# A third bank for the transposes' ring while the samples attend

## The chip, the cores and the metric

The kernel runs on one core of a Trainium2 chip. The metric is the device time of one execution in microseconds (us). Before the change three runs took 1328.84 to 1329.03 us, median 1329.01.

## The reference

One decoder layer for a prompt of 512 tokens and for 8 samples of 8 new tokens each, with shared weights and float32 throughout. What the change touches is the samples' attention over their caches: three groups of 8 heads with 64 columns, whose keys lie 1, 4 and 16 positions apart (`DILS`), so that every query sees at most 129 keys of its group.

```python
def dilated_attn_sample(q, k_new, v_new, k_buf, v_buf, dil, slopes):
    kc = jnp.concatenate([k_buf, k_new], axis=1)
    vc = jnp.concatenate([v_buf, v_new], axis=1)
    idx = buf + jnp.arange(t)[:, None] - dil * j[None, :]
    kg, vg = kc[:, idx], vc[:, idx]
    scores = jnp.einsum('bthd,btjhd->bhtj', q, kg) * (dh ** -0.5)
    scores = scores - slopes * (dil * j)
    m = jnp.max(scores, axis=-1)
    p = jnp.exp(scores - m)
    o = jnp.einsum('bhtj,btjhd->bthd', p, vg) / den
    ...
# layer:  h = adaLN-RMSNorm(x; c);  [q,k,v | u,v | gA,gB] = h @ w_in
#         A = attention of the three groups, combined by their softmax denominators
#         x = x + gate1(c) * ((sig(gA) * A @ w_pa + sig(gB) * B @ w_pb) @ w_o)
#         x = x + gate2(c) * HierMoE(adaLN-RMSNorm(x; c));  y = adaLN-RMSNorm(x; c_final)
```

## The kernel before, in words

The order of every engine's work is written out by hand, engine by engine, and semaphores tie the engines together. The stages are: adaLN and the first norm; the projections v, u, gb and pb; for each of the three head groups q, k and values of the prompt with the prompt's attention; the attention of the eight samples; the gates ga0 and ga1; pa and wo; routing; the experts; the final norm. Between the prompt's groups TensorE also computes rows of the modulation (`ada_step`, line 997) into a PSUM bank of their own, bank 5 (`ada_bank`). Their last rows (G = 3) are read by VectorE (`ada_rows`, line 2039 on) in the third group of the prompt's attention. After that bank 5 isn't used until `routed(0)` puts the first tile's routing logits there, after the samples' attention, the gates, pa and wo; later it serves `keep_warm` and the experts.

The other PSUM banks belong to two rings (`Ring`, line 176): `mm`, banks 0 to 4, for products, and `tp`, banks 6 and 7, for transposes. A ring's uses are listed ahead of the program (`stage`), each with the engine that empties it; use m has bank m modulo the number of banks. TensorE waits with `wait_empty` until the use that had the bank before, two uses back in `tp`, is emptied.

**The loads.** SyncE issues a stream of loads into four slots of 2 MB each (`SLOTS`), one load after the other in the stream's order, each when what last read its slot is done (`wait_slot_read`). For the samples the stream goes: keys of sample b in two slots (the first with 5 tiles of 128 keys in two DMAs, 256 KB and 1 MB; the second with 8 tiles in one DMA of 2 MB), then values of sample b - 1 in the same manner. The first key slot is free when key tile 4 is transposed, the second when key tile 12 is, both value slots when the previous sample's values product is done.

**The loop of the samples' attention** (line 1303 on) has ten rounds; round b takes the scores of sample b and the values of sample b - 1. `scores(b)` turns 13 key tiles (`turn_keys`, four 128x128 transposes each, recorded under line 970) and interleaves them with four score products (`quad_scores`, line 1253): key tiles 0 to 2, product 0 (key 0), tiles 3 to 6, product 1 (keys 1 to 4), tiles 7 to 10, product 2 (keys 5 to 8), the transposes of the previous sample's exponentials (lines 1235 and 1237), tiles 11 and 12, the heads of sample b - 2 (`gather_heads`, line 1299), product 3 (keys 9 to 12). `attend(b - 1)` follows (lines 1284, 1286 and 1291). In rounds 1 to 4 a tile of the prompt's output is transposed at the round's end (line 970, copied out by ScalarE at line 1546); a wait for VectorE's `combine` stands before it.

```python
            def scores(b):
                lead = (3, 7, 11, 13)
                x = 0
                for quad in range(4):
                    while x < lead[quad]:
                        if b and x == PT_AT:
                            turn_exponentials(b - 1)
                        turn_keys(b, x)
                        x += 1
                    if quad == 3 and b >= 2:
                        gather_heads(b - 2)
                    quad_scores(b, quad)
```

ScalarE copies the even key tiles out of their bank (line 169, with a small copy of the new keys ahead, line 163), VectorE the odd ones (lines 171 and 165). VectorE also places the exponentials (lines 2127 to 2130), adds the bias and takes the maxima (line 2156 on), and in rounds 1 to 4 has one step of the prompt's combination (lines 2098 to 2102) behind each of its first five key tiles. In round 0 it combines the prompt's denominators (line 2080 on), for which it waits for partial results that GpSimd loads back from DRAM (line 853). The copied key tiles stand in a ring of ten in SBUF (`KT_SLOTS`).

Of the kernel before, what the change touches and what calls it, by code (L numbers as in the profile page):

```python
# [175 lines left out]
class Ring:  # L176
# [3 lines left out]
    def __init__(self, banks, filled, emptied_act, emptied_dve):  # L180
        self.banks, self.filled = banks, filled
        self.emptied = {"act": emptied_act, "dve": emptied_dve}
        self.users, self.first = [], {}

    def stage(self, name, uses, user):
        self.first[name] = len(self.users)
        self.users += [user] * uses

    def bank(self, m):
        return self.banks[m % len(self.banks)]  # L190

    def wait_empty(self, pe, m):

        if m >= len(self.banks):
            self.wait_emptied(pe, m - len(self.banks))

    def wait_emptied(self, eng, m):

# [12 lines left out]
def build(nc, t, out):  # L211

    ctx = ExitStack()
    with ctx:
        def sem(name):
            return ctx.enter_context(nc.semaphore(name))
# [15 lines left out]
        psum = ctx.enter_context(nc.psum_tensor("psum", [P, 8, CH], F32))  # L232
# [120 lines left out]
        def rt(start, *shape):  # L353
            return at(RT0 + start, *shape)
# [8 lines left out]
        earlier, nth = rt(780, TILES + 1, 16), rt(880, TILES, 16)  # L363
# [35 lines left out]
        tp_filled, tp_act, tp_dve = sem("tp_filled"), sem("tp_act"), sem("tp_dve")  # L399
# [5 lines left out]
        ada_read, ada_out = sem("ada_read"), sem("ada_out")  # L405
# [46 lines left out]

        mm = Ring([psum[:, b, :] for b in range(5)], mm_filled, mm_act, mm_dve)
        ada_bank = psum[:, 5, :]
        tp = Ring([psum[:, b, :] for b in (6, 7)], tp_filled, tp_act, tp_dve)
        tp.stage("c", 2, "dve")
        tp.stage("h", 2 * TILES, "act")
        tp.stage("mod", 1, "dve")
# [24 lines left out]
                    mm.stage(f"o{g}{i - 2}", 1, "dve")  # L483
        PT_AT = 11
        KT_USER = ["act", "dve"] * 6 + ["act"]
        for b in range(NB + 2):
            if b < NB:
                for x in range(XT):
                    if b and x == PT_AT:
                        tp.stage(f"pt{b - 1}", 1, "dve")  # L490
                    tp.stage(f"kt{b}x{x}", 1, KT_USER[x])
                mm.stage(f"ss{b}", 1, "dve")
            if b >= 2:
                tp.stage(f"ot{b - 2}", 1, "act")
            if b == NB:
                mm.stage("ga0", TILES, "act")
                tp.stage(f"pt{b - 1}", 1, "dve")
            if 1 <= b <= NB:
                mm.stage(f"so{b - 1}", 1, "dve")
            if 1 <= b <= 4:  # L500
                tp.stage(f"o{b - 1}", 1, "act")
        mm.stage("ga1", TILES, "act")
        mm.stage("pa", 2 * TILES, "dve")
        tp.stage("shift", 3, "dve")
        tp.stage("mix", 2 * TILES, "dve")
        mm.stage("wo", 2 * TILES, "dve")
# [452 lines left out]
        def _(pe):  # L959
            used = [0]  # L960
# [53 lines left out]
            def samples_product(name, j, lhs, half):  # L1014

                n = S0[name][2 * j + half]
                slot_wait(n)
                raw, _, _ = half_slot(n)
                m = bank_of(name, j, 4)
                if half == 0:  # L1020
                    mm.wait_empty(pe, m)
                for k in range(4):
                    for out_, cols in quarters(m):
                        ins = nc.tensor.matmul(out_, lhs[:, 4 * half + k, :], raw[:, k, cols],  # L1024
                                               start=(half == 0 and k == 0), stop=(half == 1 and k == 3))
                ins.then_inc(samples_read if half == 0 else mm_filled, 1)
# [46 lines left out]
            for k in range(KD):  # L1073
                ada_step(0, k)
                if k >= KD - TILES:
                    i = k - (KD - TILES)
# [35 lines left out]
            m = tp.first["rep"]  # L1112
# [7 lines left out]
            for i in range(TILES):  # L1120
                pe.wait_ge(vn_done, i + 1)
                for half in range(2):
                    m = mm.first["sgu"] + 2 * i + half
# [134 lines left out]
# [12 lines that stand above are left out]
# [24 lines left out]
            def gather_heads(b):  # L1294
                u = tp.first[f"ot{b}"]
                mm.wait_emptied(pe, mm.first[f"so{b}"])
                tp.wait_empty(pe, u)
                for j in range(4):
                    ins = nc.tensor.matmul(tp.bank(u)[:, j * NT:(j + 1) * NT], om[:, j * P:(j + 1) * P],
                                           c_("seltok"), start=True, stop=True)  # L1300
                ins.then_inc(tp_filled, 1)

            for b in range(NB + 2):
                if b < NB:
                    scores(b)
                if b == NB:
                    samples_product("ga0", 0, h4_raw, 0)
                if b >= NB:
                    gather_heads(b - 2)
                if b == NB:  # L1310
                    samples_product("ga0", 0, h4_raw, 1)
                    project("ga0", H_PARTS, 0)
                    turn_exponentials(NB - 1)
                if 1 <= b <= NB:
                    attend(b - 1)
                if b == NB:
                    for half in range(2):
                        samples_product("ga1", 0, h4_raw, half)
                if 1 <= b <= 4:
                    pe.wait_ge(oc_done, b)  # L1320
                    transposes(tp.first[f"o{b - 1}"], 0, P, [oin[:, b - 1, k * P:(k + 1) * P] for k in range(4)])
# [7 lines left out]
            for c in range(2):  # L1329
# [9 lines left out]
                for i in range(TILES):  # L1339
                    m = mm.first["pa"] + TILES * c + i  # L1340
# [24 lines left out]
            def routed(i):  # L1365

                n, bank = ROWS[i], ada_bank
                tp.wait_emptied(pe, tp.first["z"] + Z_ORDER.index((i, 1)))
                if i:
                    mm.wait_empty(pe, mm.first["lgT"] + i - 1)  # L1370
                    bank = mm.bank(mm.first["lgT"] + i - 1)
                for step in range(2):
                    for j in range(4):
                        z = zT[:, 4 * step + j, i * P:i * P + n] if i < 4 else zT_s[:, 4 * step + j, :]
                        ins = nc.tensor.matmul(bank[32 * j:32 * j + 32, 0:n], wrt[:, 4 * step + j, :], z,
                                               start=(step == 0), stop=(step == 1))
                ins.then_inc(mm_filled if i else lgT_filled, 1)
# [16 lines left out]
            for i in range(TILES):  # L1394
# [4 lines left out]
                if i == 3:  # L1399
                    routed(0)  # L1400
            turn_z(3, 1)
            routed(1)
            routed(2)
            turn_z(4, 1)
            routed(3)
# [12 lines left out]
            m = tp.first["pos"]  # L1418
# [1070 lines left out]
```

## Time and profile before

| | |
|---|---|
| median of the runs | 1329.01 us (1328.84 to 1329.03, 3 runs) |
| span of the profiled execution, first to last instruction | 1324.4 us |
| what the median is longer than that span | 4.6 us |
| TensorE busy (matmuls) | 1241.9 us, 94% |
| VectorE, ScalarE, GpSimd busy | 660.8, 546.3, 194.4 us |
| DMA | 293.96 MB, mean 222 GB/s |
| samples' attention, rounds 0 to 7 | about 638 to 797 us of the span |

The profile is of one execution, whose own time is taken as its span; the runs' median stands beside it. A matmul's end is modelled and overlaps the next, so the distance between starts says how long a step holds TensorE. In the strip of 40 slices the DMA share is 0.9 and more in the slices of the samples' attention from 680 us on, as it is in the experts' stage; the granted TensorE clock is at least 0.9 in every slice but one, 0.7 at about 630 to 660 us, where this stage begins.

### The profile page before, as it was taken

The numbers are of one execution on the slowest core, as the hardware profiler recorded it, in microseconds if no ns is written. First come the engines' busy times: TensorE is split into PE (matmuls) and PEld (weight loads), VectorE is DVE, ScalarE is ACT, GpSimd is POOL, SyncE is SP. The second block draws the span as 40 slices with busy tenths as digits, with TensorE's granted clock in tenths as the row PEclk, the third lists the DMA queues.
The fourth block names the chain that finished last, engine by engine and source line by source line (L and its number), as shares of the span: only waits on it lengthen the run. The fifth ranks groups of instructions, "written<-read, shape, count | busy, mean of one in ns | idle before, by whom it ended". The sixth has DMA issues, their size and how long they took to land. (4 is left out here: it accounts for less than half of the span.)

```text
span 1324.4 us, 17978 instructions
## 1 busy us (share of the span) xinstructions
PE 1241.9 (94%) x7160; PEld 942.6 (71%) x7160; DVE 660.8 (50%) x920; ACT 546.3 (41%) x878; POOL 194.4 (15%) x228
## 2 busy tenths in 40 slices
PE   4899999999999999998799999999999999999987
PEld 1677877776788877886665666747757888778762
DVE  1328513223061214123466542254687888888877
ACT  3723313011372135215333333211346877777752
POOL 1203200010000010001200001100035322222220
PEclk9999999999999999999799999999989999999999
DMA  9642211263524453539679996811299999999973
GB/s 359 222 189 96 72 64 64 65 231 128 199 105 136 147 190 112 170 134 339 230 276 347 348 366 182 307 37 69 92 327 292 357 373 374 373 375 374 366 283 111
DMA packets 126235, 293.96 MB, mean 222 GB/s; under 512 B 10160, under 2 KB 10288, under 8 KB 121496
## 3 DMA queue, kind: packets, MB, share of 16 engines
q1 hardware_dynamic: 108216, 243.57, 52.2%
q0 software_dynamic: 17952, 49.44, 10.5%
q8 instruction: 49, 0.80, 0.2%
q14 instruction: 18, 0.15, 0.0%
HBM read 269.91 MB, written 30.42 MB: 227 GB/s over the span
## 5 line engine op out<-in xcount | busy, mean ns | idle before, releaser
L982 PE MATMUL psum<-part,part 128*128 128x512 f32 (+1 forms) x1088 | 441.5, 406 | 10.3 <-DVE part L1924 5.0
L983 PE MATMUL psum<-part,part 128*128 128x512 f32 (+1 forms) x1088 | 429.1, 394 | 0.0
L984 PE MATMUL psum<-part,part 128*128 128x512 f32 (+1 forms) x1088 | 429.0, 394 | 0.0
L982 PEld LDWEIGHTS psum<-part,part 128*128 128x128 f32 (+1 forms) x1088 | 227.2, 209 | 71.4 <-issue 21.8
L984 PEld LDWEIGHTS psum<-part,part 128*128 128x128 f32 (+1 forms) x1088 | 227.1, 209 | 40.2
L983 PEld LDWEIGHTS psum<-part,part 128*128 128x128 f32 (+1 forms) x1088 | 228.0, 210 | 35.9
L2342 DVE TENSOR_TENSOR part<-arena,part 128x2048 fp32r<-128x2048 f32 x96 | 219.0, 2290 | 35.0 <-ACT part L1774 33.9
L1873 DVE TENSOR_TENSOR part<-arena,part 128x2048 fp32r<-128x2048 f32 x42 | 96.3, 2301 | 252.6 <-PE psum L1024 226.3
L1774 ACT ACTIVATE part<-arena 128x2048 fp32r<-128x2048 f32 x94 | 179.7, 1920 | 44.8 <-DMA arena<-in_w_up_dram 22.5
L1546 ACT ACTIVATE arena<-psum 128x512 f32<-128x512 f32 (+3 forms) x140 | 75.7, 567 | 247.0 <-PE psum L984 202.1
L970 PE MATMUL psum<-cst,arena 128*128 128x128 f32 (+2 forms) x858 | 122.5, 283 | 40.3 <-DMA cst<-in_consts_dram 12.8
L970 PEld LDWEIGHTS psum<-cst,arena 128*128 128x128 f32 (+2 forms) x858 | 95.7, 146 | 76.5 <-issue 22.4
L1557 ACT ACTIVATE part<-arena 128x2048 fp32r<-128x2048 f32 x42 | 79.8, 1910 | 169.9 <-DMA arena<-in_w_in_dram 166.4
L1024 PE MATMUL psum<-arena 128*64 128x256 f32 x544 | 66.0, 385 | 0.1
L169 ACT ACTIVATE arena<-psum 128x512 f32<-128x512 f32 x56 | 33.4, 596 | 69.6 <-PE psum L970 69.6
L2025 DVE TENSOR_TENSOR arena<-psum,arena 128x512 f32<-128x512 f32 x30 | 19.0, 684 | 75.1 <-PE psum L1159 66.5
L1024 PEld LDWEIGHTS psum<-arena 128*64 128x64 f32 x544 | 36.1, 136 | 25.6 <-issue 8.9
L171 DVE COPY arena<-psum 128x512 f32<-128x512 f32 x48 | 33.0, 688 | 27.6 <-PE psum L970 27.5
L919 POOL DMA_INDIRECT arena<-h2d,arena x14 | 31.1, 2218 | 93.2 <-DMA arena<-slots_d 79.2
L1642 ACT ACTIVATE arena<-arena 128x128 f32<-128x128 f32 (+1 forms) x96 | 39.6, 418 | 7.4 <-DVE arena L2031 7.4
L1253 PE MATMUL psum<-arena 128*32 128x136 f32 (+1 forms) x832 | 37.9, 285 | 3.2 <-issue 1.6
L997 PE MATMUL psum<-arena 128*32 128x512 f32 x256 | 35.9, 644 | 5.3 <-DMA arena<-in_w_ada_dram 5.3
(289 smaller groups left out, 1075.0 us busy)
## 6 DMA issues: line engine op xcount, KB each, us to landing
arena<-in_w_in_dram SPq DMA_DIRECT2D x34, 1024.0 KB, 5.4
arena<-in_cache_kv_w_dram SPq DMA_DIRECT2D x16, 2048.0 KB, 11.8
arena<-in_w_gate_dram SPq DMA_DIRECT2D x32, 1024.0 KB, 9.9
arena<-in_w_up_dram SPq DMA_DIRECT2D x32, 1024.0 KB, 9.9
arena<-in_w_down_dram SPq DMA_DIRECT2D x32, 1024.0 KB, 9.8
arena<-in_w_ada_dram SPq DMA_DIRECT2D x24, 1024.0 KB, 7.6
arena<-in_cache_kv_w_dram SPq DMA_DIRECT2D x16, 1024.0 KB, 9.1
arena<-in_w_ada_final_dram SPq DMA_DIRECT2D x8, 1024.0 KB, 7.7
```

The source lines that it names most:

```text
L970: ins = nc.tensor.transpose(bank[0:a.shape[-1], k * n:k * n + a.shape[0]], a, c_("ident", a.shape[0])[:, 0:a.shape[0]])
L982: nc.tensor.matmul(out_, hi, w_hi, start=start, stop=False)
L983: nc.tensor.matmul(out_, hi, w_lo, start=False, stop=False)
L984: last_product[0] = nc.tensor.matmul(out_, lo, w_hi, start=False, stop=stop)
L1024: ins = nc.tensor.matmul(out_, lhs[:, 4 * half + k, :], raw[:, k, cols], start=(half == 0 and k == 0), stop=(half == 1 and k == 3))
L1253: ins = nc.tensor.matmul(mm.bank(m)[r, cols], Qm[:, b % 2 * 2048 + quad * 512 + j * P:b % 2 * 2048 + quad * 512 + (j + 1) * P][:, r], KT[: ...
L1546: nc.scalar.activation(dst, ring.bank(m)[0:n, 0:cols] if src is None else src, func, scale=scale).then_inc(ring.done(m), 1)
L1557: nc.scalar.activation(hi, raw, ACT.Copy).then_inc(hi_done, 1)
L1642: ins = nc.scalar.activation(sc[:, hp, 0:nk * P], sc[:, hp, 0:nk * P], ACT.Exp, bias=oe[:, job % 3, AW + hp:AW + hp + 1], accum_out=oe[:, ...
L1774: nc.scalar.activation(hi, raw, ACT.Copy).then_inc(e_hi, 1)
L1873: V.tensor_tensor(lo, raw, hi, ALU.subtract).then_inc(lo_done, 1)
L2342: V.tensor_tensor(lo, raw, hi, ALU.subtract).then_inc(e_lo, 1)
```

## The change

The ring of the transposes gets a list of banks with a turn of its own for each stage: `rotate` says which banks the next uses go round. Each use now remembers its bank and the use that had it before. For the samples' attention the turn is banks 6, 7 and 5; before and after it is 6 and 7. Two waits are added on TensorE: one ahead of the loop, for the modulation's last row (`ada_out` at 4), and one ahead of `routed(0)`, for the last use of bank 5 by the ring.

```diff
@@ -181,18 +181,29 @@
+        self.turn, self.at, self.before = list(range(len(banks))), [], []
 
     def stage(self, name, uses, user):
         self.first[name] = len(self.users)
         self.users += [user] * uses
+        for _ in range(uses):
+            b = self.turn.pop(0)
+            self.turn.append(b)
+            earlier = [m for m, used in enumerate(self.at) if used == b]
+            self.before.append(earlier[-1] if earlier else None)
+            self.at.append(b)
+
+    def rotate(self, turn):
+
+        self.turn = list(turn)
 
     def bank(self, m):
-        return self.banks[m % len(self.banks)]
+        return self.banks[self.at[m]]
 
     def wait_empty(self, pe, m):
 
-        if m >= len(self.banks):
-            self.wait_emptied(pe, m - len(self.banks))
+        if self.before[m] is not None:
+            self.wait_emptied(pe, self.before[m])
@@ -452,7 +463,8 @@
-        tp = Ring([psum[:, b, :] for b in (6, 7)], tp_filled, tp_act, tp_dve)
+        tp = Ring([psum[:, b, :] for b in (6, 7, 5)], tp_filled, tp_act, tp_dve)
+        tp.rotate((0, 1))
@@ -483,6 +495,7 @@
         KT_USER = ["act", "dve"] * 6 + ["act"]
+        tp.rotate((0, 1, 2))
         for b in range(NB + 2):
@@ -501,6 +514,8 @@
         mm.stage("pa", 2 * TILES, "dve")
+        tp.rotate((0, 1))
+        THIRD_LAST = max(m for m, used in enumerate(tp.at) if used == 2)
         tp.stage("shift", 3, "dve")
@@ -1300,6 +1315,7 @@
+            pe.wait_ge(ada_out, 4)
             for b in range(NB + 2):
                 if b < NB:
                     scores(b)
@@ -1366,6 +1382,8 @@
                 n, bank = ROWS[i], ada_bank
                 tp.wait_emptied(pe, tp.first["z"] + Z_ORDER.index((i, 1)))
+                if i == 0:
+                    tp.wait_emptied(pe, THIRD_LAST)
                 if i:
```

## Rows read from the trace of the kernel before

**Rows 1.** The page: the chain that ended last, shares of the span by engine.

```profile
PE 24%; DMA 8%; issue 2%; DVE 2%; ACT 2%; POOL 1%; SPq 0%; DVEq 0%; ACTq 0%; POOLq 0%
```

**Rows 2.** Busy time by stretch: rounds 3 and 6. Stretch, length, five engines, clock, DMA, GB/s.

```profile
719.80:739.40 19.60, 17.98 (x204) 12.12 (x201) 13.05 (x40) 7.06 (x23) 1.50 (x3) 1.00 0.98 351
...
759.00:778.00 19.00, 17.38 (x201) 11.70 (x197) 9.74 (x35) 6.58 (x22) 1.50 (x3) 1.00 0.96 346
```

**Rows 3.** Timeline of TensorE in one round: start, length, line, count, idle before and releaser.

```profile
719.75 1.09 PE L970 MATMUL psum<-cst,arena 128*128 128x128 f32 x8
721.10 1.26 PE L970 MATMUL psum<-cst,arena 128*128 128x128 f32 x8 [0.25 <-ACT arena L1546]
722.19 1.09 PE L1253 MATMUL psum<-arena 128*128 128x136 f32 x8
723.12 1.04 PE L970 MATMUL psum<-cst,arena 128*128 128x128 f32 x8
724.60 1.06 PE L970 MATMUL psum<-cst,arena 128*128 128x128 f32 x8 [0.44 <-DVE arena L171]
...
728.10 1.09 PE L970 MATMUL psum<-cst,arena 128*128 128x128 f32 x8 [0.35 <-DVE arena L171]
...
731.74 0.66 PE L970 MATMUL psum<-cst,arena 128*128 128x128 f32 x4 [0.46 <-DVE arena L2130]
732.51 1.03 PE L1299 MATMUL psum<-cst,arena 128*128 128x8 f32 x8
...
734.53 1.12 PE L1284 MATMUL psum<-arena 128*128 128x512 f32 x2
...
739.36 0.87 PE L970 MATMUL psum<-cst,arena 128*128 128x128 f32 x6
```

**Rows 4.** Groups by line, 680.5 to 797: count, busy, mean ns, idle before and its releasers.

```profile
L970 PE MATMUL psum<-cst,arena 128*128 128x128 f32 x328 | 46.2, 279 | 9.1 <-DVE arena L171 4.7 <-DVE arena L2130 2.8 <-ACT arena L1546 1.1
```

**Rows 5.** Timeline of VectorE in the same round.

```profile
723.76 0.69 DVE L171 COPY arena<-psum 128x512 f32<-128x512 f32 x1 [0.46 <-PE psum L970]
724.37 0.68 DVE L2098 TENSOR_TENSOR arena<-arena 128x512 f32<-128x512 f32 x1
725.08 0.18 DVE L165 COPY arena<-arena 128x32 f32<-128x32 f32 x1
725.26 0.69 DVE L171 COPY arena<-psum 128x512 f32<-128x512 f32 x1
...
730.88 0.28 DVE L2127 COPY arena<-psum 24x128 f32<-24x128 f32 x1 [0.80 <-PE psum L1237]
...
731.41 0.27 DVE L2130 COPY arena<-psum 128x32 f32<-128x32 f32 x2
```

**Rows 6.** Busy time by stretch, columns as in rows 2: parts of a round, and round 1's beginning.

```profile
723.00:734.00 11.00, 9.64 (x139) 7.96 (x141) 7.39 (x19) 3.76 (x11) 0.00 (x0) 1.00 1.05 384
735.00:739.00 4.00, 4.00 (x28) 0.97 (x26) 3.07 (x17) 1.38 (x7) 0.00 (x0) 1.00 1.04 396
...
739.50:743.00 3.50, 3.25 (x27) 2.83 (x27) 1.55 (x4) 2.03 (x6) 1.49 (x3) 1.00 0.73 204
...
660.00:675.00 15.00, 12.51 (x136) 10.23 (x140) 11.08 (x31) 5.11 (x17) 0.00 (x0) 0.80 0.56 187
```

**Rows 7.** Waits of SyncE's queue, 680.5 to 797: total us, times, longest.

```profile
SPq L711 <- PE psum L970: 49.2, 10, 7.3
SPq L711 <- PE psum L1291: 39.7, 6, 6.7
```

**Rows 8.** DMA of 719.8 to 739.4; the load issued at 732.4 (duration ns; to landing).

```profile
DMA packets 3509, 6.87 MB, mean 351 GB/s; under 512 B 168, under 2 KB 168, under 8 KB 3507
...
L711 SPq DMA_DIRECT2D arena<-in_cache_kv_w_dram x1: 379/379/379, 732.4 to 732.4; - x1
...
DMA to landing us min/median/max: 10.1/10.1/10.1
```

**Rows 9.** Timelines of VectorE and of TensorE, end of round 0 and in round 1.

```profile
656.69 0.26 DVE L2080 TENSOR_REDUCE arena<-arena 128x32 f32<-128x96 f32 x1 [3.46 <-DMA arena<-oscr]
...
663.03 0.68 DVE L171 COPY arena<-psum 128x512 f32<-128x512 f32 x1
...
660.88 1.11 PE L970 MATMUL psum<-cst,arena 128*128 128x128 f32 x4 [4.99 <-ACT arena L169]
...
674.59 1.13 PE L1253 MATMUL psum<-arena 128*32 128x136 f32 x32 [0.78 <-ACT arena L169]
```

**Rows 10.** The chain that ended last, in order of time: start, length, what.

```profile
797.04 1.88 PE psum L1024 x16
...
827.30 2.71 PE psum L1291 x24
```

## The prediction

> **What bounds the kernel now.** I read the page first. The chain that ended last is TensorE above all, then DMA [rows 1], so a wait of TensorE is worth its length only where no transfer ends it. Then the stretches, one for each round of the sample attention (one sample's scores, the previous sample's values) [rows 2]: a round takes 19.6 us while samples still carry a prompt tile and a combination, and 19.0 us in the last two of the six shown. In every one the DMA share is 0.96 to 0.99 at 346 to 353 GB/s. TensorE and DMA are therefore both nearly full, and the question is which of them gives way.
>
> TensorE in one round [rows 3]: the key tiles come in pairs, and nearly every pair after the first is held by a copy out of its bank (0.25, 0.44, 0.35, 0.46 us in brackets; counted by starts it is more, since a matmul's modelled end hangs over). In the six rounds these waits belong to the transposes, and none of them is on a DMA [rows 4]. VectorE's copy of a key tile takes 0.69 us and, with a combination (0.68) and a small copy (0.18) behind it, the next starts 1.50 us later at the earliest: 723.76 to 725.26 [rows 5]. Then DMA: for eleven microseconds of a round it moves 384 GB/s, for four more 396, and for 3.5 us around the round's end only 204 [rows 6]. That hole has a cause: the values of the next sample may only be issued when the last values matmul is done, and by then the queue has run dry. SyncE waits for TensorE at both kinds of slot [rows 7]. One round moves 6.87 MB; its last transfer, the second half of the keys, is issued at 732.4 and lands 10.1 us later [rows 8].
>
> **The change, part by part.** It removes no instruction and adds none that computes; it moves the point at which a transpose may start from "two uses ago is emptied" to "three uses ago".
>
> TensorE's own round with three banks, walked from the rows. Passes of a transpose start 0.11 apart (4 to a tile, so 0.44 a tile). The parts: 15 groups (one prompt tile, 13 key tiles, the exponentials) at 0.44 = 6.6; the first score product 0.93 (8 passes, it begins at 722.19 and the next transposes at 723.12); three others at 1.06 = 3.2 (heads and last score product fill 732.51 to 734.53, 2.02, of which the heads 0.96); values 4.83 (734.53 to 739.36) [rows 3]. Sum 16.5. The waits that I find left when each transpose waits for the third use back: about 0.1 before the first score product (copy of key 0), 0.04 at key 6 and 0.1 at key 10 (VectorE's 1.50 us pace), 0.2 at the heads (they now wait for the exponentials' three copies, which end 0.8 us after they begin [rows 5]), 0.2 of switching. So 17.2 us against 19.6: 2.4 less. Without prompt tile and combination it is 16.6 against 19.0, again 2.4. The two ways agree: what the two banks cost now, by starts, is 0.43 + 0.11 + 0.61 + 0.51 + 0.63 + 0.27 = 2.56 us a round.
>
> First two rounds, ahead of those in [rows 2]. In round 0 the tiles come some 1.1 us sooner, but VectorE stands until 656.69 for the partial results that it combines, and TensorE behind it for 4.99 us: that gain is worth nothing. The load of values 0 moves forward by the same 1.1 us beside those partial results; it queues behind a load already running, so I take no cost, at worst 0.6 us (half of 1.1, two queues sharing). In round 1 the third key tile is transposed already when the stall ends, which saves 0.9 us at half clock (1.11 us for its four passes, against 0.66 for four elsewhere [rows 3]); from 663.03 on VectorE's 1.50 pace sets the tiles, and quad 3 of that round, now at 674.59, comes at about 672.5 [rows 9]. Round 1 ends 2.0 us sooner, at 678.5.
>
> If TensorE alone decided, rounds 2 to 7 would give 6 x 2.4 = 14.4 more, 16.4 in all. DMA does not let it. At full rate a round's bytes take 6.87 MB / 388 GB/s = 17.7 us (388 between the 384 and 396 of rows 6), longer than 17.2 and 16.6. So the bound changes hands: with the values issued earlier the 3.5 us hole closes, and the keys' second half becomes late; TensorE waits for it at key 5, 3.7 us into a round. The sum by transfers: values 1 are issued at 678.5 and move from 680.0 (as now, 1.5 later: rows 6 have the dip right behind the issue). Five rounds' loads, values 1 to keys 7, end at 680.0 + 5 x 17.7 = 768.5. The last one lands some 2.5 us behind its last packets (now: dry at about 739.5, landed at 732.4 + 10.1 = 742.5 [rows 6, 8]), at 771.0. Key 5 stands 3.7 us into round 7, so round 7 begins at 767.3 instead of 778.0: 10.7 gained. Round 7 itself has only two 1 MB weight loads behind its values, so TensorE's 16.6 against 19.0 holds there: 2.4 more. **Together 13.1 us**.
>
> The Trainium skill speaks against even this: DMA: Bandwidth & Descriptors (Where 436 GB/s comes from) says that for transfers from HBM the HBM side binds at about 358 GB/s a core. By it a round would need 6.87/0.358 = 19.2 us and the whole gain would be about 5.6 us. This trace disagrees, with 384 GB/s over eleven microseconds and 396 over four; the page HBM Reference itself sets that share for two cores streaming at once, and here one runs.
>
> The two new waits. The one for the modulation's last row ahead of round 0: the rows are added by VectorE before it adds the biases of the last two prompt tiles, whose values TensorE has already waited for. Zero; were that order gone, one VectorE instruction of 0.7 us. The one ahead of the first routing product is on a copy over 50 us old: zero, else a 0.69 us copy. Back to two banks: the first transposes behind the loop already wait for the last heads' copy. Zero. No DMA is added, and SyncE's order stays.
>
> What comes behind round 7 is a chain of TensorE work without a fixed date: weights there and in the experts are issued when slots are read [rows 10]. I pass all of the 13.1 on; a clock dip that falls otherwise is 1 to 2 us either way.
>
> The profiled execution has a span of 1324.4; the runs' median is 1329.01, 4.6 longer, for what lies around the span. 1324.4 - 13.1 = 1311.3, plus 4.6: **1315.9 us**. About 0.2%, 2.7 us, is what a measurement here tells from no change.
>
> **The rivals.**
> A, transfers were the bound all along: the hole is only paid back, the mean rate stays at 351 over a whole round. Then a round takes 6.87/0.351 = 19.5, round 7 begins at 680.0 + 97.5 + 2.5 - 3.7 = 776.3, 1.7 sooner, and with 2.4 the gain is 4.1: 1324.9. For it: 0.98 share. Against: 384 to 396 held for 15 us. Chance 0.1; in sizes between A and the forecast (a rate of 370, rounds of 18.5, gain 9) another 0.1: 1320.
> B, transfers do not bind, since the last landing shrinks once the queue stays full: TensorE's 16.4, 1312.6. Chance 0.1.
> C, it does not do what it says: the copies' pace, not the bank, holds the tiles. VectorE is busy 13.05 us of a round and ScalarE 7.1 [rows 2], and VectorE's copy starts behind a wait for TensorE (0.46 us at 723.76), so neither is full. Gain under 2.7: 1328. Chance 0.05.
> D, slower: TensorE's waits, now spread as 0.5 us pieces, bunch into one long wait for keys. The 5 us stand at 656 to 661 is followed by passes at twice the length and a mean clock of 0.80 in 660 to 675 [rows 6, 9]. A round at half clock costs about 12 us more (its 11.7 us of passes other than values double). It decides from a wait of about 5 us a round; two such rounds give back 24 against 16 gained: 1337. Chance 0.04.
>
> **How the numbers follow.** Forecast 0.6, between 1313.5 and 1318.5; B 0.1, the sizes between 0.1, A 0.1, C 0.05, D 0.04, the rest anything. The range takes the forecast, B and the sizes between: 1311.5 to 1322. Faster by over 0.2%: 0.91; within: 0.05; slower: 0.04.
>
> **What the changed profile would show.** Rounds of 17.5 to 17.9 us; no wait for VectorE or ScalarE before the transposes but at key 6, key 10 and the heads; a wait on DMA, some 0.5 us a round (1 in round 6), before the transposes, where there is none now; DMA share near 1.04 over whole rounds at 380 GB/s or more and no 204 hole; round 7 of 16.6; the stretch behind it unchanged in length. Rounds of 19 with 350 GB/s would make A right; rounds of 17.2 with no DMA wait, B; waits for VectorE as long as now, C.

## The result, and the profile after

Four runs of the changed kernel have a median of 1318.66 us (1314.65 to 1320.52), beside 1328.92 (1328.56 to 1329.03) of the kernel before on the same chip: a ratio of 0.993, with a 95% interval of 0.991 to 0.9949. It is faster by 10.3 us. The forecast was 1315.9, with a range of 1311.5 to 1322.0: the sign and the mechanism hold, the time is 2.8 us longer than forecast, just outside the 1313.5 to 1318.5 that had the chance of 0.6.

The page of the changed kernel, as in [rows 1], with its head:

```profile
span 1313.0 us, 17979 instructions
...
PE 78%; DMA 11%; DVE 4%; ACT 4%; issue 2%; POOL 2%; SPq 0%; DVEq 0%; ACTq 0%; POOLq 0%
```

The chain's shares are not like those of [rows 1]: where two engines run level, following each instant back to "what came last" tips from one to the other on small differences. I draw nothing from it. The rounds say more. Busy time by stretch of the changed kernel, rounds 2 to 7, with the columns of [rows 2] (stretch, length, five engines, clock, DMA share, GB/s):

```profile
679.30:697.00 17.70, 17.55 (x201) 12.17 (x202) 12.91 (x40) 7.06 (x23) 1.50 (x3) 1.00 0.98 350
697.00:715.00 18.00, 17.64 (x201) 12.23 (x202) 12.93 (x41) 7.07 (x23) 1.50 (x3) 1.00 1.05 383
715.00:732.60 17.60, 17.45 (x201) 12.12 (x201) 12.91 (x40) 7.07 (x23) 1.50 (x3) 1.00 1.05 384
732.60:750.30 17.70, 17.55 (x201) 12.21 (x202) 9.75 (x35) 7.18 (x24) 1.49 (x3) 1.00 1.05 382
750.30:769.20 18.90, 16.94 (x197) 11.68 (x197) 9.74 (x35) 6.58 (x22) 1.50 (x3) 1.00 1.05 384
769.20:787.00 17.80, 17.12 (x201) 11.87 (x200) 9.12 (x28) 8.17 (x22) 5.76 (x9) 1.00 1.04 376
```

In the second to the fifth of them the DMA rate is 382 to 384 GB/s over whole rounds, where [rows 2] had 346 to 351 (round 7, with fewer loads behind it, has 376). Five rounds of six take 17.6 to 18.0 us instead of 19.6, or of 19.0 in round 7; round 6 takes 18.9 instead of 19.0. (By these ends of rounds the first line of [rows 2] is round 4, not round 3; the second is round 6.) The same view of the 3.5 us around the end of round 4, where [rows 6] had 204 GB/s, shows that the hole is gone:

```profile
731.50:735.00 3.50, 3.46 (x32) 2.33 (x25) 2.47 (x8) 1.77 (x5) 1.49 (x3) 1.00 1.05 386
```

Next TensorE's groups by line in these six rounds, the line that answers to [rows 4]:

```profile
L985 PE MATMUL psum<-cst,arena 128*128 128x128 f32 x328 | 42.4, 277 | 2.6 <-DMA arena<-in_cache_kv_w_dram 2.6
```

The same 328 transposes were held for 9.1 us, by copies of VectorE and ScalarE; now they are held for 2.6 us, and only by DMA. The timeline shows one round of TensorE (answering to [rows 3]) and then the three places in rounds 6 and 7 that matter:

```profile
714.85 2.00 PE L985 MATMUL psum<-cst,arena 128*128 128x128 f32 x16
716.89 1.17 PE L1268 MATMUL psum<-arena 128*128 128x136 f32 x8
717.89 2.04 PE L985 MATMUL psum<-cst,arena 128*128 128x128 f32 x16
719.86 1.13 PE L1268 MATMUL psum<-arena 128*32 128x136 f32 x32
...
732.50 2.00 PE L985 MATMUL psum<-cst,arena 128*128 128x128 f32 x16
...
752.61 1.04 PE L985 MATMUL psum<-cst,arena 128*128 128x128 f32 x8
...
755.49 1.09 PE L985 MATMUL psum<-cst,arena 128*128 128x128 f32 x8 [1.84 <-DMA arena<-in_cache_kv_w_dram]
...
773.19 1.09 PE L985 MATMUL psum<-cst,arena 128*128 128x128 f32 x8 [0.56 <-DMA arena<-in_cache_kv_w_dram]
```

Four tiles (16 passes) now run without a wait for a copy. Rounds 4 and 5, of 17.65 us, have no wait on DMA at all. The three waits that there are come in round 3 (0.2 us), in round 6, the first whose own work is 0.6 us shorter (1.84 us in one piece), and at key 5 of round 7. SyncE still waits for TensorE at both kinds of slot, as in [rows 7]; the waits of its queue, 680 to 790:

```profile
SPq L726 <- PE psum L1306: 40.0, 6, 6.7
SPq L726 <- PE psum L985: 39.6, 10, 6.2
```

Last, the load of keys 7's second half, which answers to [rows 8]:

```profile
L726 SPq DMA_DIRECT2D arena<-in_cache_kv_w_dram x1: 379/379/379, 762.2 to 762.2; - x1
...
DMA to landing us min/median/max: 10.9/10.9/10.9
```

To compare executions I use two lengths. **Rounds 0 and 1** run from round 0's first score product to the last values matmul of round 1; **rounds 2 to 7** from there to round 7's last values matmul. Before: 642.38 to 680.54 (38.2 us), then 116.5, to 797.04. After: 643.66 to 679.26 (35.6), then 107.7, to 786.92. So 10.1 of the 11.4 us by which the spans differ are there at the end of round 7; behind it lie 527.4 us before and 526.1 after, a difference within what single executions vary by (see the sum, below).

### The profile page after: what moved, and what is told of

Read it like the earlier page. It is cut to its first block, busy times and chain, and to the rows that moved or that the text cites. A ratio compares the mean times of both kernels' runs of the same rounds, so it can differ in the third digit from the quotient of the medians.

```text
span 1313.0 us, 17979 instructions
## 1 busy us (share of the span) xinstructions
PE 1237.6 (94%) x7160; PEld 941.9 (72%) x7160; DVE 661.7 (50%) x920; ACT 548.7 (42%) x878; POOL 194.0 (15%) x228
## 4 chain that ended last, share of the span: by engine, by line
PE 78%; DMA 11%; DVE 4%; ACT 4%; issue 2%; POOL 2%; SPq 0%; DVEq 0%; ACTq 0%; POOLq 0%
PE psum L997 18%; PE psum L999 17%; PE psum L998 17%; PE psum L985 5%; PE psum L1039 5%; DMA arena<-in_cache_kv_w_dram 3%; DMA arena<-in_w_gate_dram 2%; PE psum L1360 2%; PE psum L1196 2%; PE psum L1012 2%; DMA arena<-in_w_ada_dram 2%; PE psum L1268 2%; ACT arena L1564 1%; POOL slots_d L915 1%; PE psum L1174 1%
## 5 line engine op out<-in xcount | busy, mean ns | idle before, releaser
L985 PE MATMUL psum<-cst,arena 128*128 128x128 f32 (+2 forms) x858 | 117.7, 282 | 26.9 <-DMA cst<-in_consts_dram 12.4
L950 POOL DMA_INDIRECT yd<-arena x15 | 32.4, 2161 | 98.3 <-issue 91.5
```

The source lines that it names most:

```text
L985: ins = nc.tensor.transpose(bank[0:a.shape[-1], k * n:k * n + a.shape[0]], a, c_("ident", a.shape[0])[:, 0:a.shape[0]])
```

## The experiments

Times are medians in us beside the kernel before on the same chip; its own runs had a median of 1325.9 on the chip of after_again to light_after (1323.2 to 1331.34, 23 runs), 1327.86 on that of third_start to later_after (1323.81 to 1332.01, 17 runs), 1326.15 on that of the last four of the table (1322.01 to 1332.01, 23 runs). The three columns at the right come from each kernel's profile; the clock is the granted clock from 655 to 680.

| run | median | ratio, 95% | rounds 0, 1 | clock | rounds 2 to 7 |
|---|---|---|---|---|---|
| before | 1328.92 | 1 | 38.16 | 0.86 | 116.5 |
| after | 1318.66 | 0.993 [0.991, 0.9949] | 35.60 | 0.93 | 107.7 |
| after_again | 1318.51 | 0.9946 [0.9928, 0.9965] | 36.83 | 0.86 | 107.8 |
| waits_only | 1327.63 | 1.0011 [0.9996, 1.0026] | 38.39 | 0.86 | 116.5 |
| light_before | 1326.38 | 1.0006 [0.9992, 1.002] | 38.49 | 0.86 | 116.5 |
| light_after | 1313.4 | 0.9895 [0.987, 0.992] | 37.28 | 0.86 | 104.8 |
| third_start | 1326.63 | 0.9987 [0.9974, 1.0] | 36.85 | 0.86 | 117.3 |
| third_rest | 1321.24 | 0.9944 [0.9917, 0.9971] | 39.08 | 0.86 | 109.1 |
| later_before | 1322.99 | 0.9961 [0.9949, 0.9974] | 35.25 | 0.93 | 116.6 |
| later_after | 1314.18 | 0.9885 [0.9865, 0.9904] | 32.55 | 0.93 | 108.1 |
| third_five | 1318.61 | 0.9939 [0.9925, 0.9952] | 35.60 | 0.93 | 107.7 |
| later_again | 1313.76 | 0.9909 [0.9885, 0.9933] | 34.42 | 0.93 | 108.5 |
| heavy_before | 1328.32 | 1.0012 [1.0, 1.0025] | 37.50 | 0.93 | 116.5 |
| heavy_after | 1330.02 | 1.0019 [1.0003, 1.0036] | 36.84 | 0.86 | 114.8 |

**after_again**, the changed kernel as it is, on another chip.

> The changed kernel once more, five rounds, to see why its four runs spread over 5.9 us (1314.65 to 1320.52) where those of the kernel before lie within 0.5. Theory T1 (the bound has moved from TensorE's ring to the transfers; the rest of the spread is clock): rounds 3 to 5 of the samples' attention take 17.65 to 17.95 us again, in every profile, and the runs' spread goes with their mean granted clock (0.977 to 0.982 so far, each 0.001 about 1.3 us of span at half speed, so 0.65 us or more). Rival T2 (the transfers themselves are unsteady now that they are the bound): the rounds differ by 1 us and more from one profile to the next, and the clock stays within 0.001.

Rounds 2 to 7 take 107.8 us, as in the first profile, and rounds 3 to 5 17.77 to 17.93, within what was expected. Rounds 0 and 1 are 1.2 us longer at a lower clock. The other half of the expectation isn't borne out: over these six runs the time doesn't go with the mean clock (correlation -0.1). The gain by medians is 7.4 us here.

**waits_only**, the change's new waits and its book-keeping, but two banks:

```diff
-        tp.rotate((0, 1, 2))
+        tp.rotate((0, 1))
...
-        THIRD_LAST = max(m for m, used in enumerate(tp.at) if used == 2)
+        THIRD_LAST = len(tp.users) - 1
```

> Two banks as before, with the two new waits of TensorE (for the modulation's last row and for an old copy ahead of the first routing product). T1: the waits cost nothing and bring nothing: within 0.05% of the kernel before, 1329 us, rounds of 19.6 and 19.0 us. Rival: a wait moves TensorE's clock windows or costs an issue each: up to 1 us slower.

The rounds are those of before to the hundredth (19.6 and 19.0), and the interval of the ratio spans 1. The third bank alone does it; the two waits cost nothing in the samples' rounds, and nothing that the medians can tell (1.7 us more, inside their interval).

**light_before and light_after**: four of the eight far value tiles of every sample are not loaded, 1.05 MB a round less (6.87 to 5.83 MB). The instructions of the engines stay. What the samples put out from those tiles isn't the reference's.

```diff
-                [(slice(0, 8), keys_of(b, kv, 2))])
+                [(slice(0, 8), keys_of(b, kv, 2))] if kv == 0 else [(slice(0, 4), keys_of(b, kv, 2)[:, 0:4, :])])
```

> The kernel before, with only 4 of the 8 far value tiles of each sample loaded (1 MB instead of 2; the other four keep older data, so the samples' output is left uncomputed in part). A round then moves 5.8 MB instead of 6.9. T1: two banks bound the rounds, not DMA, so they stay at 19.6 and 19.0 us, with a DMA share near 0.83, and the time stays within 1 us of 1329. Rival A of the prediction (transfers were the bound all along): rounds fall to 16.5 us or to TensorE's 17, and the time by 10 us or more.

> The changed kernel with the same lighter value loads. A round's bytes take 5.8 MB / 387 GB/s = 15.0 us, so with three banks TensorE decides: T1 expects rounds of 17.2 us with prompt tile and combination and 16.6 to 17.0 without, no wait on DMA before the transposes, and a time some 3 us under the changed kernel (five rounds 0.5 shorter, plus the waits of rounds 5 to 7 that add up to 2.5). Rival C (the copies' pace holds the tiles): the rounds stay at 17.7 and over, with waits for VectorE.

Busy time by stretch, round 4 of light_before, then round 4 of light_after:

```profile
720.60:740.20 19.60, 17.98 (x201) 12.11 (x202) 13.05 (x40) 7.07 (x23) 1.50 (x3) 1.00 0.82 297
```

```profile
716.20:733.80 17.60, 17.45 (x202) 12.12 (x201) 12.92 (x40) 7.06 (x23) 1.50 (x3) 1.00 0.92 331
```

With two banks a round takes 19.6 us at a DMA share of 0.82 as it did at 0.98: transfers did not bind the kernel before. With three banks and slack transfers the rounds are TensorE's own: 17.66 with prompt tile and combination, 17.05 without, and the view of waits has none of TensorE for VectorE or ScalarE in them. They sum to 104.8, against 107.7 with all the bytes: that is what transfers hold in the changed kernel, 2.9 us in six rounds. By medians light_after is 13.0 us below light_before. TensorE's round in light_after:

```profile
716.13 2.00 PE L985 MATMUL psum<-cst,arena 128*128 128x128 f32 x16
718.17 1.17 PE L1268 MATMUL psum<-arena 128*128 128x136 f32 x8
719.17 2.04 PE L985 MATMUL psum<-cst,arena 128*128 128x128 f32 x16
721.14 1.13 PE L1268 MATMUL psum<-arena 128*32 128x136 f32 x32
722.21 2.10 PE L985 MATMUL psum<-cst,arena 128*128 128x128 f32 x16
724.24 1.13 PE L1268 MATMUL psum<-arena 128*32 128x136 f32 x32
725.30 0.55 PE L1250 MATMUL psum<-cst,arena 128*128 128x128 f32 x3
725.68 0.27 PE L1252 MATMUL psum<-cst,arena 128*24 128x128 f32 x1
725.79 1.04 PE L985 MATMUL psum<-cst,arena 128*128 128x128 f32 x8
726.95 1.03 PE L1314 MATMUL psum<-cst,arena 128*128 128x8 f32 x8
...
728.97 1.12 PE L1299 MATMUL psum<-arena 128*128 128x512 f32 x2
```

Four tiles take 1.97 to 2.04 from start to start (716.13 to 718.17, 719.17 to 721.14, 722.21 to 724.24), not 4 x 0.44 = 1.76. The tiles themselves keep to 0.44: the eight passes at 725.79 last 1.04, which is seven steps of 0.11 and the last pass's 0.27, across the boundary of two tiles. The rest stands at the ends of the groups: the fourth tile of the first group, by a narrower window of the same timeline, starts at 717.50, and the score product 0.67 behind it.

```profile
717.50 0.63 PE L985 MATMUL psum<-cst,arena 128*128 128x128 f32 x4
```

**third_start and third_rest** split the change in time: the third bank in rounds 0 and 1 alone, or from round 2 on alone.

```diff
+            if b == 2:
+                tp.rotate((0, 1))
```

```diff
-        tp.rotate((0, 1, 2))
...
+            if b == 2:
+                tp.rotate((0, 1, 2))
```

> Third bank in rounds 0 and 1 alone, two banks from round 2 on. The prediction's first term by itself: from round 0's first score product to round 1's end 38.2 to 38.5 us with two banks, 35.6 to 37.3 so far with three. T1: about 36.8, rounds 2 to 7 at 116.5 as with two banks, so 1.3 to 2 us gained in all. Rival: the stand of round 0 swallows all of it, 38.3.

> Third bank from round 2 on alone. T1: 38.3 us to round 1's end, then rounds 2 to 7 at 107 to 108 us in all: the two halves of the change add up, since the transfers start later with round 1's end and so don't catch up. Rival: as the transfers bind the last rounds, what the first rounds lose is made up there, and rounds 2 to 7 take 106.5 or less.

third_start brings 1.3 us less in rounds 0 and 1 and gives 0.8 of it back: where the ring changes, a bank comes up that ScalarE is still emptying. third_rest has a wait of the same length at its own change, and the transfers hold TensorE in round 4 (that they are still late from two slower rounds is my reading; no run shows it). The timelines, first of third_start, then of third_rest:

```profile
681.14 1.07 PE L987 MATMUL psum<-cst,arena 128*128 128x128 f32 x8 [0.84 <-ACT arena L1566]
```

```profile
683.80 1.39 PE L986 MATMUL psum<-cst,arena 128*128 128x128 f32 x11 [0.84 <-ACT arena L1565]
...
724.33 1.09 PE L986 MATMUL psum<-cst,arena 128*128 128x128 f32 x8 [1.78 <-DMA arena<-in_cache_kv_w_dram]
```

From the first score product to the end of round 7 the two take 154.1 and 148.2 us, against 154.7 before and 143.3 with the change: 0.5 and 6.5 saved apart, 11.4 together (10.0 in after_again). Against after_again, whose clock was the same, the two parts fall 3.0 us short of the whole. Of this the two switches in mid-flow, which the change itself doesn't pay, are 1.7; and rounds 0 and 1 of third_rest, which run the code of before, took 0.6 to 0.9 us longer than in the other runs with two banks at that clock. So third_rest's expectation (38.3 and then 107 to 108) was missed on both counts, and whether the halves add up but for the switches isn't shown. Most of the gain is from round 2 on.

**later_before and later_after, later_again**: the combination of the partial results starts one round later, in round 1 instead of 0, and ends one later (and so do the turned tile and the exponentials that feed it). later_before has two banks, the other two (one kernel, on two chips) have three.

```diff
-                        if b == 0 and x == 11:
+                        if b == 1 and x == 11:
...
-                        if 1 <= b <= 4 and x < 10:
-                            combine(b - 1, x // 2)
+                        if 2 <= b <= 5 and x < 10:
+                            combine(b - 2, x // 2)
...
-                if 1 <= b <= 4:
-                    turn_in(tp.first[f"o{b - 1}"], 0, P, oT[:, :, (b - 1) * P:b * P])
+                if 2 <= b <= 5:
+                    turn_in(tp.first[f"o{b - 2}"], 0, P, oT[:, :, (b - 2) * P:(b - 1) * P])
```

> The same move in the kernel before, with two banks. T1: round 1 ends 5 to 6 us sooner, rounds 2 to 7 stay at 19.6 and 19.0 (116.5 in all) since the ring holds them, total 5 to 6 us under the kernel before. Rival: as in the run above, under 2 us.

> The changed kernel with the whole combination of the prompt's groups one round later (differences of the maxima and weights in round 1, a step of the combination and the turned prompt tile in rounds 2 to 5 instead of 1 to 4). Nothing is left out. VectorE then has no wait for the partial results in round 0, on which TensorE stands about 5 us and after which its clock is at half speed for 3.4 to 6.8 us. T1 (transfers set the last rounds, so what is won ahead of round 2 moves the transfers too): round 1 ends 5 to 6 us sooner, counted from round 0's first score product (31 instead of 36 to 37 us), rounds 2 to 7 keep 107 to 108 us in all, total 5 to 6 us under the changed kernel. Rival (the transfers have no room left: values 0, landed at 671.7, and keys 2 are then late): the stand comes back as a wait on DMA in rounds 1 and 2, and the gain is under 2 us.

> The changed kernel with the combination one round later, five rounds. T1: the 4 us that it won ahead of round 2 (32.6 instead of 36.8 us to round 1's end) stay, so 4 us under the changed kernel, ratio to the kernel before 0.989 to 0.991. Rival: it was the draw of the four runs, and the two kernels agree within 1.5 us.

This goes at what the third bank could not touch, the stand in round 0. TensorE's timeline there, of the changed kernel and then of later_after:

```profile
661.91 2.15 PE L1268 MATMUL psum<-arena 128*128 128x136 f32 x8 [5.12 <-ACT arena L169]
```

```profile
658.26 1.26 PE L1268 MATMUL psum<-arena 128*128 128x136 f32 x8 [2.47 <-ACT arena L169]
```

The stand halves and the first matmuls behind it take 1.26 instead of 2.15 us. By medians later_before is 4.9 us below before, with an interval that excludes 1, and later_again 4.9 below third_five (1313.76 and 1318.61, same chip), though their intervals overlap and its six runs lie apart (three at 1311.4 to 1311.7, one at 1315.8, two at 1318.5 and 1320.0). The profiles show less than the 5 to 6 us expected: among runs with a clock of 0.93, rounds 0 and 1 shorten by 2.3 us with two banks (35.25 and 37.50) and by 3.1 and 1.2 with three (32.55, 34.42 and 35.60). So that the move helps is shown with two banks; with three the size stays open. Rounds 2 to 7 do not shorten further (108.1 and 108.5), since there the transfers hold: TensorE waits for them from round 2 on. Timeline of later_after:

```profile
680.55 1.10 PE L985 MATMUL psum<-cst,arena 128*128 128x128 f32 x8 [0.39 <-DMA arena<-in_cache_kv_w_dram]
...
699.09 1.09 PE L985 MATMUL psum<-cst,arena 128*128 128x128 f32 x8 [0.79 <-DMA arena<-in_cache_kv_w_dram]
```

**third_five**, the changed kernel once more, on the chip of later_again.

> The changed kernel, five rounds on the same chip as the next run, for a direct comparison. Expected as before: 7 to 10 us under the kernel before (ratio 0.9925 to 0.9947), 107 to 108 us from round 1's end to round 7's in the profile, with the last three of these rounds held by the transfers.

1318.61 against 1326.15 is 7.5 us. Rounds 2 to 7 are 107.7 again, but the longest wait for DMA, 1.33 us, is in round 5, before TensorE's round gets shorter, and not in round 6. Timeline of third_five:

```profile
738.75 1.09 PE L985 MATMUL psum<-cst,arena 128*128 128x128 f32 x8 [1.33 <-DMA arena<-in_cache_kv_w_dram]
```

**heavy_before and heavy_after**: two more far value tiles are loaded with each sample's values, into room that nothing reads: 0.52 MB a round more, 7.39 in all.

```diff
+            more = [(slice(5, 7), more_of(b, kv))] if kv else []
-            put(f"{'KV'[kv]}{b}", last, [(slice(0, 1), keys_of(b, kv, 0)), (slice(1, 5), keys_of(b, kv, 1))],
+            put(f"{'KV'[kv]}{b}", last, [(slice(0, 1), keys_of(b, kv, 0)), (slice(1, 5), keys_of(b, kv, 1))] + more,
```

> The kernel before with the same two more value tiles. 19.1 us of transfers fit under its 19.6 us rounds as far as rate goes, but the keys' second half had 1.7 us to spare and moves back by 1.35: T1 expects rounds of 19.6 to 19.8, a share near 1.03 without the hole at the round's end, and the time within 1.5 us of the kernel before. Rival: the ring and the loads add up, rounds of 20.5 to 21.

> The changed kernel with two more far value tiles loaded per sample into unused room of a slot, which nothing reads (0.5 MB, one DMA more). A round then moves 7.39 MB, at 387 GB/s 19.1 us. T1 (the bound is now the transfers): rounds 3 to 6 go from 17.7 to about 19.1 us, with waits on DMA before the transposes and a share of 1.05, and the stage gets 7 us longer. Rival (TensorE's order still bounds, the two only lie close): rounds of 17.7 to 18.

Busy time by stretch, a round of heavy_before, then rounds 4 and 5 of heavy_after:

```profile
720.00:739.60 19.60, 17.98 (x204) 12.13 (x200) 13.05 (x41) 7.07 (x23) 1.50 (x3) 1.00 1.03 378
```

```profile
715.90:735.70 19.80, 17.62 (x202) 12.21 (x202) 13.02 (x40) 7.07 (x23) 1.50 (x3) 1.00 1.05 382
735.70:754.80 19.10, 17.59 (x201) 12.18 (x202) 9.75 (x35) 7.18 (x24) 1.49 (x3) 1.00 1.05 382
```

Two banks carry 0.52 MB more in the same 19.6 us: the former hole takes it. With three banks the same bytes need 7.39 MB / 382 GB/s = 19.3 us, rounds 3 to 5 are 19.1 to 19.8 (round 2 is 17.7 still, round 6 22.0), and TensorE waits for DMA before the transposes (the view of waits, 679 to 795: total, times, longest):

```profile
PE psum L991 <- DMA arena<-in_cache_kv_w_dram: 8.1, 4, 3.3
```

The longest of the four ends at 761.46, and there the granted clock falls, first the wait in TensorE's timeline of heavy_after, then the stretch behind it by busy time:

```profile
761.46 1.63 PE L991 MATMUL psum<-cst,arena 128*128 128x128 f32 x8 [3.29 <-DMA arena<-in_cache_kv_w_dram]
```

```profile
761.46:766.00 4.54, 4.54 (x48) 3.62 (x49) 0.97 (x3) 0.72 (x2) 0.00 (x0) 0.62 1.06 388
```

A mean of 0.62 over 4.54 us is 3.4 us at half speed ((1 - 0.62) / 0.5 x 4.54), which costs 1.7 us of passes. That is rival D's mechanism at work, behind a wait of 3.3 us where I had put its beginning at 5.

The third bank's gain is gone but for 1.7 us of rounds 2 to 7, and the runs show none of it: heavy_after's median is 1.7 above heavy_before's, and 11.4 above third_five's, where rounds 2 to 7 account for 7.1. The rest arises behind round 7, in the stretch of 537.1 us (530.7 in heavy_before, 526.0 to 530.9 in all other runs): the loads are late there too. Timelines of TensorE, heavy_before and then heavy_after, and the busy time by stretch behind the second wait:

```profile
803.45 1.73 PE L1030 MATMUL psum<-arena 128*64 128x256 f32 x14 [2.24 <-DMA arena<-in_w_in_dram]
```

```profile
800.84 3.68 PE L1045 MATMUL psum<-arena 128*64 128x256 f32 x16 [4.18 <-DMA arena<-in_w_in_dram]
```

```profile
800.84:806.00 5.16, 5.16 (x20) 2.99 (x21) 1.36 (x1) 3.93 (x4) 0.00 (x0) 0.50 1.06 363
```

TensorE waits for a weight load, 4.18 us in heavy_after, and runs the next 5.2 us at half clock. Neither before nor the three profiles of the changed kernel have such a wait. The bank's worth hangs on the bytes: 11.7 us in rounds 2 to 7 with 5.83 MB a round, 8.8 with 6.87, 1.7 with 7.39.

## Why the prediction was right, and where it was off

**The bound changes hands: right.** Rounds of 17.5 to 17.9 were forecast, and five of six come out at 17.65 to 17.94; the hole is gone, and the waits for copies have given way to waits for DMA. Transfers were not the bound before (rival A: light_before), nor were the copies' pace (rival C: light_after's rounds are shorter and wait for no copy). The sizes between A and the forecast started from a mean rate near 370; it is 382 to 384.

**The page's rate: wrong here.** By the Trainium skill, DMA: Bandwidth & Descriptors (Where 436 GB/s comes from), rounds could not go below 19.2 us. They take 17.7, at 382 to 384 GB/s held for whole rounds. That share, as the page HBM Reference of the Trainium skill (Specifications) puts it, is for two cores streaming at once, which no run here had.

**TensorE's own walk was 0.46 too short.** Forecast: 17.2 and 16.6 us; measured with slack transfers: 17.66 and 17.05 (light_after). The 0.44 a tile holds. What was too small is the terms for waits and switching, 0.64 in all. Read pass by pass from light_after's round 4, the steps longer than the plain 0.11 add up to 1.18: 0.27 around the first score product (put at 0.1), 0.12 each at keys 6 and 10 (0.04 and 0.1), 0.28 before the heads (0.2), and 0.39 at the other changes of tile or product (0.2). What each of these steps waits for the profile doesn't say: its view of waits has none there. "The two ways agree" was no check: the count of 2.56 us took as lost to two banks all that exceeds 0.11 at a held step, but the step before the heads is 0.39 with three banks as with two. The ring of two cost 19.60 - 17.66 = 1.94.

So TensorE (17.66) and DMA (6.87 MB / 384 GB/s = 17.9) run nearly level, not 0.5 apart, and the wait doesn't show as 0.5 a round: by starts it is 0.30 in round 3, nothing in rounds 4 and 5, 1.93 in round 6 and 0.65 in round 7, together the 2.9 by which light_after is shorter. My sign for it ("some 0.5 us a round, 1 in round 6") was wrong in that. Where it gathers differs between executions (round 5 in third_five), and why there isn't shown. Rival B, TensorE alone, put 14.4 us of gain in rounds 2 to 7 by the short walk; light_after, with the true walk, shows 11.7. The transfers take 2.9 of that.

**Rounds 2 to 7 gained 8.8, not 11.1.** By the steps: "five rounds' loads end at 680.0 + 5 x 17.7" used 388 GB/s. The trace of after moves 33.99 MB in the 89 us from 681 to 770:

```profile
681.00:770.00 89.00, 86.23 (x991) 59.62 (x990) 57.94 (x190) 34.06 (x114) 6.53 (x14) 1.00 1.05 382
```

At 382, five rounds take 89.9 instead of 88.5. From round 1's end at 679.26, the 1.5 behind the issue, 89.9 and the 2.5 of landing give 773.2; it landed at 762.23 + 10.9 = 773.1. The landing comes 3.9 into round 7, not 3.7: round 7 begins 1.2 us later than forecast, counted from round 1's end. Round 7 itself was to take 16.6 and took 17.70: 0.46 from the walk and 0.65 from the wait for key 5 (0.56 in brackets, 0.65 against light_after's 17.05). That wait is a slip of the sum. Its 3.7 is where key 5 stands in a round with a prompt tile; round 7 has none, and TensorE is at key 5 after 3.2 us by the same walk, after 3.3 in the trace. The forecast let round 7 begin 3.7 before the landing and then run without a wait. Together 2.3.

**Rounds 0 and 1: 2.0 forecast, 1.6 to 1.9 measured at equal clock.** In the profiles the granted clock from 655 to 680 takes one of two values, 0.86 or 0.93, whatever the kernel. At 0.93 two banks take 37.5 (heavy_before) and three take 35.6 (after, third_five); at 0.86 two banks take 38.2 to 39.1, three 36.8 to 37.3, by medians 38.4 and 36.8. The two groups of clock lie 0.9 to 1.2 us apart, though the stand in round 0 differs too (5.12 us in after, 5.71 in after_again). The first profiles fell on either side (before 0.86, after 0.93), so the 2.6 they show flatters the change. The forecast's reading of round 0, that sooner tiles are worth nothing since VectorE stands, is right: the stand is 5.12 us, as 4.99 before. I had noted that it stays, but not that it was the next thing to remove: it was (later_after).

**The waits: right, zero** (waits_only). Rival D did not come with the change's own bytes, where the longest wait is 1.84 and the clock stays at 1.00; but heavy_after shows that it is nearer than I had it: 0.52 MB more a round bunch the waits to 3.3 us, and to 4.2 us behind the loop, and half clock follows each. Its price is 1.7 us for the first and some 2.6 for the second (half of the 5.2 us), not the 12 of a whole round at half clock.

**The sum.** The end of round 7 was forecast at 797.04 - 13.1 = 783.9 and stands at 786.92: 2.3 of the 3.0 from rounds 2 to 7, 0.8 from round 1's end (679.26, not 678.5; round 0 began 1.3 later, and it was 2.6 shorter). The other profiles of the changed kernel have it at 787.5 and 787.8, a gain of 9.2 to 10.1. The medians give 10.3, 7.4 and 7.5 on three chips. The changed kernel is the same on all three (1318.66, 1318.51, 1318.61); it is the kernel before that differs, 1328.92 in four runs and 1325.9 and 1326.15 in 23 each. So 7.4 to 7.5 rests on more runs than 10.3, and whether the first four were a draw or the chip stays open. In the profiles the stretch behind round 7 is 526.1, 529.0 and 526.0 us, 527.4 and 526.6 with two banks (before, waits_only), so no loss shows there beyond the spread of single runs. "Pass all of the 13.1 on" is compatible with it, not shown; heavy_after shows that it fails once the loads run late.

**"4.6 for what lies around the span" was wrong, and it helped the forecast.** In the runs with a profile, the time is 1.7 above the span (1314.65 and 1313.0; 1318.23 and 1316.5 in after_again). The profile of before was thus an execution of some 1326.1, 2.9 below the three runs shown. With 1.7 in place of 4.6 the forecast would have been 1313.0, 5.7 us below the result instead of 2.8: that it came as near as it did is in part luck. The spread of those three, 0.2 us, was not typical: on the other chips the same kernel ran between 1322 and 1332. For the kernel before, an execution's mean clock (0.974 to 0.985) goes with its time only in part (correlation -0.4 to -0.7 on the three chips); what the rest is stays open. The forecast should have asked what an 0.2-us spread over three runs is worth.

## What to carry to other kernels

Counting the waits that a third buffer takes away gives an upper bound; what is left of them is decided by the resource next in line, so work out its round as well, in bytes over the rate that the same trace holds in its fullest stretch, and expect that where the two come out level the wait may gather in one place. Removing bytes and adding bytes that nothing reads are two cheap edits that show how far apart the two are, and in which kernel. Before a difference of a few us in one stretch is put down to an edit, compare the granted clock of that stretch in both profiles.

## What the runs showed of the hardware

- This kernel's one core streamed at a mean of 382 GB/s, with a DMA share of 1.05, for 89 us on end (382 to 384 over single rounds); I had taken 388 from shorter stretches.
- Inside a run of transposes the passes start 0.11 us apart, across the boundary of two tiles too (eight passes in 1.04 us); where TensorE goes over to or from another kind of product, and around keys 6 and 10, single steps are 0.16 to 0.39. That adds up to over 1 us of a 17.66-us round (light_after), and it isn't shown as idle time.
- A stand of TensorE of 3.29 us was followed by 3.4 us at half the clock (1.2 GHz for 2.4), one of 1.84 by none. A stand's length alone doesn't settle it: behind one of 2.47 us in round 0 the granted clock from 660 to 665 is 0.74 in later_after and 1.00 in later_again, the same kernel (there 0.66 comes later, from 670 to 675).
- The same kernel's executions on one chip spread over 10 us (23 runs, 1322.01 to 1332.01), and in the stretch from 655 to 680 one execution of the changed kernel was granted a clock of 0.86 and two 0.93.
